# Two hybrid layers: norm factors applied after the input products, window attention woven between the latent heads, and a reordered end of the layer

## The reference

```
def hybrid_layer(x, norm_g, w_in, ...):
    h = rms_norm_2(x, norm_g)
    proj = h @ w_in
    (q_lat, kv_lat, k_rope, g_mla, c_h, c_b, c_c, g_conv, s_q, s_k, s_v, g_swa) = split(proj)
    y_mla  = mla_mixer(q_lat, kv_lat, k_rope, ...) * silu(g_mla)             # 8 causal heads
    y_conv = short_conv_mixer(c_h, c_b, c_c, conv_w) * silu(g_conv)          # b * conv3(c * h)
    y_swa  = swa_mixer(s_q, s_k, s_v, q_norm, k_norm, sinks) * silu(g_swa)   # 4 blocks of 128 queries
    return x + concatenate([y_mla, y_conv, y_swa]) @ w_out
```

## Time and profile before

| what | us |
|---|---|
| three runs | 1617.04, 1622.49 (median), 1625.16 |
| the profiled execution, time | 1620.2 |
| the profiled execution, span from first to last instruction | 1618.4 |
| mean granted PE clock | 0.962 of full |
| PE busy in the span | 1483.0 |

### The profile page before, as it was taken

One profiled execution on the slowest core, in us unless ns is written; L12 is line 12 of the kernel. 1 busy time (PEld: TensorE's weight loads), 2 busy tenths in 40 slices (PEclk: granted clock), 3 DMA queues, 4 the chain that ended last, 5 costly groups with the idle time before them and its releaser, 6 DMA issues.

```text
span 1618.4 us, 23623 instructions
## 1 busy us (share of the span) xinstructions
PE 1483.0 (92%) x10032; PEld 1153.0 (71%) x10032; DVE 802.2 (50%) x1255; ACT 584.1 (36%) x1012; POOL 270.1 (17%) x225
## 2 busy tenths in 40 slices
PE   5999697987899999999989899998898899998899
PEld 3777576875678888888866687767686678776677
DVE  7766856244543323323364655457544555546652
ACT  4365231245342222222223434233623344333441
POOL 0000223101001101100012324322201332232210
PEclk9999898989999999999989999999998999999999
DMA  9239143521222223233221121111122112211122
GB/s 356 84 108 123 57 147 131 161 92 40 78 74 96 91 94 102 91 124 95 100 80 53 39 79 65 66 53 53 52 91 98 40 52 79 65 66 52 52 70 86
DMA packets 51368, 143.11 MB, mean 88 GB/s; under 512 B 13248, under 2 KB 17984, under 8 KB 50496
## 3 DMA queue, kind: packets, MB, share of 16 engines
q1 hardware_dynamic: 51264, 141.60, 27.5%
HBM read 136.90 MB, written 4.69 MB: 87 GB/s over the span
## 4 chain that ended last, share of the span: by engine, by line
PE 75%; DVE 11%; ACT 7%; issue 4%; POOL 2%; DMA 1%; SPq 1%; POOLq 0%; DVEq 0%; ACTq 0%
PE b L401 73%; ACT arena L2155 4%; DVE arena L1267 2%; PE b L404 2%; DVE arena L1275 2%; DVE arena L2118 1%; POOL arena L2802 1%; ACT tile L2158 1%; ACT ring L2158 1%; DVE X L1267 1%; DVE tile L1267 1%; DVE ringr L1267 1%; DVE arena L1943 1%; DMA arena<-scr_yd 1%; DMA cst<-in_cst 1%
## 5 line engine op out<-in xcount | busy, mean ns | idle before, releaser
L401 PE MATMUL b<-tile,ring 128*128 128x512 f32 (+1 forms) x1840 | 662.2, 399 | 13.4 <-ACT tile L2158 7.7
L401 PE MATMUL b<-HR,ring 128*128 128x512 f32 (+1 forms) x944 | 389.7, 413 | 37.5 <-DVE arena L1267 12.4
L401 PEld LDWEIGHTS b<-tile,ring 128*128 128x128 f32 (+1 forms) x1840 | 347.7, 190 | 101.4 <-issue 20.3
L1267 DVE TENSOR_TENSOR ringr<-ring,ring 128x1024 fp32r<-128x1024 f32 x186 | 254.8, 1374 | 246.7 <-ACT ring L2158 245.7
L401 PE MATMUL b<-HR,ringr 128*128 128x512 f32 (+1 forms) x944 | 375.0, 397 | 0.0
L401 PE MATMUL b<-arena 64*64 64x64 f32 (+10 forms) x3104 | 231.4, 289 | 32.9 <-issue 10.8
L2158 ACT ACTIVATE ring<-ring 128x1024 fp32r<-128x1024 f32 x186 | 195.0, 1054 | 161.4 <-DMA ring<-in_ws 161.4
L401 PEld LDWEIGHTS b<-HR,ring 128*128 128x128 f32 (+1 forms) x944 | 180.5, 191 | 88.7 <-issue 22.4
L401 PEld LDWEIGHTS b<-arena 64*64 64x64 f32 (+5 forms) x3104 | 151.5, 153 | 101.2 <-issue 71.4
L401 PEld LDWEIGHTS b<-HR,ringr 128*128 128x128 f32 (+1 forms) x944 | 179.9, 191 | 46.0 <-issue 0.3
L401 PE MATMUL b<-tile,ringr 128*128 128x512 f32 x448 | 178.6, 399 | 0.0
(11 more groups left out here) (123 smaller groups left out, 1205.3 us busy)
## 6 DMA issues: line engine op xcount, KB each, us to landing
ring<-in_ws SPq DMA_DIRECT2D x218, 512.0 KB, 3.5
arena<-in_ws SPq DMA_DIRECT2D x15, 512.0 KB, 15.3
arena<-in_lw SPq DMA_DIRECT2D x2, 1280.0 KB, 6.2
X<-in_xT SPq DMA_DIRECT2D x2, 1024.0 KB, 6.1
arena<-scr_kpad SPq DMA_DIRECT2D x8, 256.0 KB, 11.8
X<-in_xT SPq DMA_DIRECT2D x1, 2048.0 KB, 8.3
outT<-X SPq DMA_DIRECT2D x8, 256.0 KB, 3.0
arena<-in_cst SPq DMA_DIRECT2D x1, 1088.0 KB, 5.9
```

The source lines that it names most:

```text
L401: return self.e.matmul(out, lhsT, rhs, start=start, stop=stop, skip_group_check=True)
L1267: return self.e.tensor_tensor(out=out, in0=a, in1=b, op=op)
```

## The change

It touches only the end of the first block and the two layers.

- **Late norm.** `Hs` is now X times gain only, without the token's factor. `high` (ACT) and `lower` (DVE) make it tile by tile while the preceding output product still runs. PE starts `latents` at once: rows 0 to 3, then `token_sums`, rows 4 to 7, then `spread`. DVE works out the factors (`token_factors`), ACT copies the spread factors from PSUM to SBUF (`factors`: RR, and RF in layer 0). The factor is applied to the projections instead: gate tiles 8 to 11 while DVE evicts them, the values in ACT's copy, the rope part on DVE, and on POOL, as a new `scaled` product of 128x512 by RR, the gate tiles 0 to 7 (once each), conv tile CH (twice each, four tiles) and YC (once each, four tiles): 20 POOL products a layer. Where norms follow, the epsilon is scaled (`e2`). In layer 0 DVE also multiplies the eight X tiles by `fgain` and RF after the latents (`residual`).
- **Woven attentions.** The steps of `windows` are written out in `WINDOW` and mixed with `heads` and `dense_rest` by the string `LAYER`. Buffers ZZ, WP and SO move into the space of heads that are done (`HOME`, `BEFORE`). In `heads`, the reciprocal on DVE and the scaling on POOL move one step later.
- **End of the layer.** All eight gates 4 to 11 are one step on ACT; Y 4 to 7 are split during the first two `begin_out` steps; the output products of rows 4 to 7 for tiles 0 to 3 are a piece of their own ("middle", four steps) behind `begin_out`, and the last loop has rows 8 to 11 only.

The core of the diff:

```diff
+LAYER = ("qqqd" * 4 + "q" + "hd" * 9 + "hdx" * 3 + "hd" + "hdx" * 5 + "hd" + "hdxx" * 2 + "hdx" + "hdxx" + "hdxy" + "dx"
+         + "xddxdxdd" + "dddd")
+WINDOW = "a0 b0 r0 t0 s0 a1 b1 r1 t1 s1 a2 b2 r2 a3 b3 t2 r3 s2 t3 s3".split()
+HOME, BEFORE = [0, 0, 1, 0], [None, 0, None, 1]
...
 # PE, latents
-        self.dense_rows([(self.name, n) for n in range(4)], ready, [128, 128, 128, 32])
+        self.dense_rows(tiles, ready, M, range(4))
+        for name in names:
+            self.token_sums(name)
+            self.give((name, "sums"), (nd, (name, "mean")))
+        self.dense_rows(tiles, ready, M, range(4, 8))
+        for name in names:
+            self.spread(name)
+            self.give((name, "spread"), (na, (name, "R")))
...
 # PE, end of dense_rest
         for n in range(4):
-            self.begin_out(f"o{l}", n, k.Y[:4], range(4), each)
+            self.begin_out(o, n, k.Y[:4], range(4), each[:4])
+            yield
+        for n in range(4):
+            self.dense(("middle", o, n), [(o, n, r) for r in range(4, 8)], k.Y[4:8], k.bank[o, n][:, :], each[4:],
+                       start=False, stop=False)
             yield
...
 # DVE
+    def lower(self, name, r, gain):
+        self.wait_ge(k.s("norm_act"), (name, "hi", r))
+        hi, lo = k.Hs[r]
+        self.stt(lo, k.Xk[r], gain, hi.bitcast(F32), ALU.mult, ALU.subtract).then_inc(*k.s("norm_dve").inc((name, "lo", r)))
...
+    def residual(self, r):
...
+        self.stt(X, X, k.pc("fgain", r), k.RF, ALU.mult, ALU.mult).then_inc(*k.s("norm_dve").inc(("f", "x", r)))
...
 # ACT
+    def high(self, name, r, gain, *when):
...
+        self.af(k.Hs[r][0], k.Xk[r], ACT.Copy, scale=gain).then_inc(*k.s("norm_act").inc((name, "hi", r)))
+    def factors(self, name, dst):
+        self.wait_ge(k.s("norm_pe"), (name, "spread"))
+        self.cp(dst, k.bank[name, "spread"][:, :]).then_inc(*k.s("norm_act").inc((name, "R")))
...
-        self.gates(l, range(4, 8))
-        for m in range(4, 8):
-            self.out_split(l, m)
-        yield
-        for n in range(4):
+        self.gates(l, range(4, 12))
+        yield
+        for n in range(8):
             self.blocks(4)
+            if n < 2:
+                self.out_split(l, 4 + 2 * n)
+                self.out_split(l, 5 + 2 * n)
             yield
...
 # POOL, dense_rest
+        def scaled(x, source, raw, event):
+            self.wait_ge(source, raw)
+            self.wait_ge(k.s("norm_act"), ("l1" if l else "g", "R"))
+            self.tt(x, x, k.RR, ALU.mult).then_inc(*pool.inc(event))
+        for n in range(4):
+            scaled(k.G[:, n, :], act, (l, "g", n), (l, "g", n))
+            yield
...
         for j in range(4):
+            if j:
+                scaled(k.G[:, 3 + j, :], act, (l, "g", 3 + j), (l, "g", 3 + j))
+            scaled(k.CH, act, (l, "ch", j), (l, "ch1", j))
+            scaled(k.CH, pool, (l, "ch1", j), (l, "ch", j))
             yield
             self.wait_ge(dve, (l, "cu", j))
             self.ts(k.YC[:, j, :], k.CU[:, 0:512], k.pc(f"cw{l}", j), ALU.mult).then_inc(*pool.inc((l, "tap", j)))
             yield
             yield
+            scaled(k.YC[:, j, :], dve, (l, "yc", j), (l, "ys", j))
             yield
+        scaled(k.G[:, 7, :], act, (l, "g", 7), (l, "g", 7))
```

More of the change, by code:

```diff
@@ L997, in layer @@
         self.latents(l)
[L998 to L1001, removed]
+        self.play(LAYER, q=self.qk(l), h=self.heads(l), x=self.windows(l), d=self.dense_rest(l))
         act, dve, pool = k.s("y_act"), k.s("y_dve"), k.s("y_pool")
@@ L1006, in layer @@
             if n < 4:
-                self.dense((o, n), [(o, n, r) for r in range(4, 12)], k.Y[4:], k.bank[o, n][:, :], each[4:], start=False)
+                self.dense((o, n), [(o, n, r) for r in range(8, 12)], k.Y[8:], k.bank[o, n][:, :], each[8:], start=False)
             else:
@@ L2123, in A, with R @@
             self.tt(es, sink, mx, ALU.subtract).then_inc(*dve.inc((l, "es", n)))
+        def R(n):
+            mx, nm, rs, es, rc = (S[:, HOME[n], i, :] for i in range(5))
             self.wait_ge(act, (l, "es", n))
@@ L2558, in layer, with head_splits @@
         self.latents(l)
-        rest = self.dense_rest(l)
-        self.weave((self.qk(l), 3), (self.some(rest, 4), 1))
-        self.weave((self.heads(l), 1), (self.some(rest, 19), 1))
+        self.play(LAYER, q=self.qk(l), h=self.heads(l), x=self.windows(l), d=self.dense_rest(l), y=self.head_splits(l))
+        for m in range(8, 12):
+            self.out_split(l, m)
+    def head_splits(self, l):
         for m in range(4):
             self.out_split(l, m)
-        self.weave((self.windows(l), 2), (rest, 1))
-        self.gates(l, range(8, 12))
-        for m in range(8, 12):
-            self.out_split(l, m)
+        yield
     def out_split(self, l, m):
@@ L2592, in latents @@
         name = f"l{l}"
-        self.dense_tiles(4, self.norm_apply("l1") if l else self.norm_two_rows())
+        self.ahead()
+        for r in range(8):
+            self.blocks(4)
+            if r == 4 and l:
+                self.norm_root("l1", k.r_)
+            elif r == 4:
+                self.norm_root("f", k.r_)
+                self.norm_root("g", k.r2_)
+        if not l:
+            self.factors("f", k.RF)
+        self.factors("l1" if l else "g", k.RR)
         for n in range(3):
@@ L3142, in layer @@
             self.blocks(8)
-        for n in range(4):
+        for n in range(8):
             self.blocks(4)
         for n in range(8):
-            self.blocks(8 if n < 4 else 12)
+            self.blocks(4 if n < 4 else 12)
             if l:
```

428 lines of the change are left out of this document (221 added, 207 removed).

## The result

| | before | after |
|---|---|---|
| median of the runs, us (6 each) | 1622.38 | 1610.95 |
| lowest and highest | 1617.04 to 1625.16 | 1609.05 to 1616.92 |
| profiled execution, us (span) | 1620.2 (1618.4) | 1611.2 (1609.4) |

The changed kernel takes 0.9937 of the time before, with a 95% interval of 0.9918 to 0.9957. It is faster, as forecast, but by 11 us where the sum had 32, and its 1611 lies above the range's 1606. The forecast time was 1588. So the question of this case is where 23 us went.

What follows compares the result with a forecast made beforehand. PE, busy 92% of the span, bounds the kernel, so only its idle and low-clock time can be won. 17.4 + 2 x (17.7 - 1.5 - 1.1 - 7.0) = 33.6, less 1.6, gives 32: 1588 us, range 1571 to 1606.

Steps and rivals of the forecast that it cites:

- Late norm: Last down or output product to first qk product: 32.0 in layer 0, 29.1 in layer 1; both gain 17.6, 17.4 kept.
- rival 3: Both layer starts: longer tail behind the latents and extra work cancel the early start; 1605; chance 0.24 shared with rival 2.
- qk: qk part: new POOL product per gate tile holds DVE, delaying three rounds by 0.5 each; costs 1.5 a layer.
- Waits that go: Woven attentions: waits of 2.77, 4.65, 4.53, smaller ones and the low clock behind them vanish; 17.7 a layer.
- Cost 1.1 a layer, bounds 0.8 and 3: Window transposes and value product standing together: the product waits for ACT's copy of the last transposes and a hand-over.
- 7 a layer; bounds 1 and 10: End of layer: PE waits 2.5 before window 3's transposes, 2.8 before its value products, plus 1.7 of low clock.
- Rival 1: End of the layer is covered after all, costing 1 to 2; gain 42 to 44, time 1577; chance 0.16.
- 9.6 less predicted in each: Each layer's net gain from the woven attentions and layer end, without the qk charge.
- the general 0.8 that I had taken off: Per-layer share of the 1.6 taken off the sum for the residual's thin cover and tight banks.
- rival 2: Window part: chains meet in queues, PE waits 1.5 to 2 at most steps; 1604; chance 0.24 shared with rival 3.
- Rival 4: POOL's 20 new products hold DVE, leaving PE short of `w_lo`; decides from 35 us, up to 1640, slower; chance 0.06.

Runs made afterwards that it cites:

- the repaired one: Changed kernel with window 1's value products one step later, gate 7 scaled before window 3's product, gates behind window 3's transposes, ACT's eviction before factor copies: 1590.88, ratio 0.9810.
- products and writes: Kernel with all four order repairs (products, 1590.88) against the same with POOL's 20 new products a layer replaced by constant writes, scaling left out: 1579.24, ratio 0.9732.

## Why the prediction was wrong

**Late norm: right.** From the last down product to the first qk product it said 32.0 and 29.1; the profile has 32.0 (817.17 to 849.20) and 29.7. The tail behind the latents, longer because ACT is serial, was seen, and the run with ACT's eviction first gave back 4 of it (its interval overlaps with the changed kernel's). That answers rival 3.

**qk: too low by 1.9 in all.** It said 1.5 a layer; from the first qk product to the first of `heads` it is 1.9 more than before in layer 0 and 3.0 in layer 1. One part is what I named, the bank wait of 2.77 (0.7 more). The other I had left out: behind the tail the first twelve products run at a low clock (0.57 in layer 0). They took 7.5 and 6.9, before the change 6.3 and 4.6. I had costed the tail as time alone.

**Waits that go: right as to which, and the price was not the failure.** None of the three long waits of the earlier trace rows is in the profile after; what took their place is the next two points.

**"Cost 1.1 a layer, bounds 0.8 and 3" for s1: the step that failed.** It measured 7.2, a wait of 4.05 and some 3.2 of low clock. I priced it as a hand-over from ACT's copy. What came last was DVE's copy, at the end of a chain through three queues that PE's work did not cover. DVE held by POOL is 2.1 us of that chain: with the new products cut short 2.21 of the 4.05 remain. Moving s1 by one step returned 11 us, of the 12.2 that this term missed in two layers.

**End, "7 a layer; bounds 1 and 10": a size.** It measured 10.0: waits of 1.19, 3.94 and 2.40 and about 2.5 of low clock. Two of the places were as said (the 1.19 before s2 was not) and so was what released t3, but POOL's window product began 21.4 behind b3 and not 18.7, and s3 waited for DVE and not for ACT, since DVE's four gated products took 7.17. Rival 1, an end that is covered, fell; an output piece more moved the wait to the next place each time.

These two terms miss 6.1 and 3.0 a layer. From the first head product to the end of the output product the kernel took 302.7 and 302.5 before, 304.2 and 304.1 after, against 9.6 less predicted in each; less the general 0.8 that I had taken off, 10.3 are missing. The remaining 1.2 I read as product time: attention's float32 products, without the transposes, add up to 50.7 before and 55.6 after in layer 0, 3.2 of that added by the low clock behind s1's wait. More changes between the two kinds of product would do it; no run isolates it.

**The cause under both: an order too tight for its queues, and POOL's twenty products.** The runs show two losses that add. Mending the order gave 20 us with the products in place (22 where they are cut short); cutting the products short gave 17 in the changed kernel and 20 in the repaired one. Together they are 40 us: the 23 missed, and most of the 19 that the forecast had itself charged for qk, s1 and the end. Neither alone covers it.

The first loss is rival 2's, chains that meet in the queues. I had followed the banks and the units of cover, and not what each step's last copy has ahead of it on its own engine. For the second, the forecast charged POOL's twenty products 1.5 a layer in qk and nothing in the woven part, because DVE had 100 us spare. Rival 4 had the effect, at 35 us to decide and 6%, but by another path: PE short of `w_lo` once DVE is two units behind. No wait of PE in the two layers was released by a weight split. What cost time were small DVE steps in the attention's chains, held till a POOL product ended, and POOL's own queue ahead of window 3's product. The rival's argument against itself, that half of DVE's instructions read PSUM or a single tile, failed too: the 128x4 operation reads a single tile and was held. By its busy time DVE was held for 15.0 in all in the changed kernel, where the rival's bound was 54.8.

The Trainium skill ("SBUF — State Buffer", section "Who interferes with whom") says that a DVE instruction with two SBUF inputs is held by a GpSimd one that reads SBUF, and not by one that only writes it: the 128x8 rows, 1.25 beside a product and 0.16 beside a write, agree. The 128x4 operation has one SBUF input, so that sentence does not cover it.

**What stays open.** How much of the 12 us between products and writes is holding and how much the slightly shorter occupancy (1.3 against 1.5 each) isn't separated. Nor is the low clock: the same waits without it were not tried. Whether the woven order gains anything over the old one isn't shown either, since no run had the old order of the windows with the late norm.

## What to carry to other kernels

An engine's spare time did not tell here what a step in a chain would wait for. When work is given to POOL, look for the DVE instructions between two engines of a chain, however small, and charge each with the rest of the POOL instruction that it can meet. In a woven order, follow for each consumer every copy that it needs, on each queue with what stands ahead, and leave one more step between a transpose and its use; that one step was worth 11 us here. A wait that is taken away at the end of a chain is only gone when the run shows that no neighbour has grown: two attempts with an output piece more moved it whole, and scaling gate 7 first moved a part of it.

## What the runs showed of the hardware

- A DVE operation on 128x4 elements, 0.17 alone, took 1.76 and 2.42 us, each time till the end of a POOL product with SBUF inputs that ran beside it; POOL's writes of a constant didn't lengthen a 128x8 operation (0.16, against 1.25 beside a product).
- Behind an idle time of 4.05 us the granted clock was 0.76 over 13 us, so the 16 records behind it cost 3.2 us more: nearly the wait again.
- Behind the latents, where PE ran only small products, twelve qk products took 6.8 us at clock 0.57; in layer 1 of the kernel before, the clock at the same place was 1.00. The same instructions of layer 0's start ran at 0.78 in one profile and 1.00 in another.
